# Scaling and adding 32 gathered rows on GpSimd instead of VectorE in a fused expert block

## What is computed

```python
q = (xb @ w_query).reshape(PEER_TOKEN_BLOCK, PEER_HEADS, 2, D_KEY // 2)
...
sc, ci = lax.top_k(cand, PEER_TOPK)
e = (jnp.take_along_axis(i1, ci // PEER_TOPK, axis=-1) * N_KEYS
     + jnp.take_along_axis(i2, ci % PEER_TOPK, axis=-1))
g = jax.nn.softmax(sc, axis=-1)
u = expert_u[e]
act = jax.nn.gelu(jnp.einsum('td,thkd->thk', xb, u).astype(jnp.float32))
return jnp.einsum('thk,thkd->td', (g * act).astype(xb.dtype), expert_v[e])
```

## Time and profile before

| what | value |
|---|---|
| median of 3 runs | 1208.1 us (1206.0 to 1208.2) |
| the profiled execution's own time | 1209.2 us |
| its span, first to last instruction | 1207.1 us |
| PE busy over the span | 98% |
| DVE, ACT, POOL busy over the span | 63%, 58%, 61% |
| the down product | about 547 to 882 us |
| in it: PE, DVE, ACT, POOL busy | 329.1, 238.7, 177.1, 91.1 of 335 us |
| granted TensorE clock in it | 1.00 (the upper level, 2.4 GHz) |

### The profile page before, as it was taken

One profiled execution on the slowest core, in us unless ns is written; L12 is line 12 of the kernel. 1 busy time (PEld: TensorE's weight loads), 2 busy tenths in 40 slices (PEclk: granted clock), 3 DMA queues, 4 the chain that ended last, 5 costly groups with the idle time before them and its releaser, 6 DMA issues.

```text
span 1207.1 us, 24649 instructions
## 1 busy us (share of the span) xinstructions
PE 1179.2 (98%) x8981; PEld 1111.7 (92%) x8981; DVE 759.0 (63%) x1516; ACT 704.3 (58%) x1370; POOL 741.8 (61%) x349
## 2 busy tenths in 40 slices
PE   7999999999999999999999999999999999999997
PEld 6888999999999999999899999999999988899896
DVE  4454059995007778885777777777647746457446
ACT  5585445556558888775555555555564666456554
POOL 7747868888887777774232232331057776677674
PEclk9999999999999999999999999999999999999999
DMA  6735545665554444457778778777665434454443
GB/s 243 264 122 192 179 139 193 203 203 198 199 203 169 168 170 167 165 174 274 251 264 270 262 254 272 249 255 256 195 236 192 140 126 137 140 203 149 136 158 108
DMA packets 67145, 237.68 MB, mean 197 GB/s; under 512 B 8912, under 2 KB 10360, under 8 KB 66688
## 3 DMA queue, kind: packets, MB, share of 16 engines
q1 hardware_dynamic: 57024, 206.14, 50.9%
q0 software_dynamic: 7392, 25.68, 5.9%
q10 hardware_dynamic: 2656, 4.90, 1.1%
HBM read 232.30 MB, written 6.31 MB: 198 GB/s over the span
## 4 chain that ended last, share of the span: by engine, by line
PE 82%; DMA 5%; DVE 4%; ACT 4%; POOL 2%; issue 2%; DVEq 0%; SPq 0%; ACTq 0%
PE W L581 29%; PE W L825 6%; PE A L825 6%; PE A L625 5%; PE A L632 5%; PE A L627 5%; DMA ring<-exp_v 4%; PE A L827 3%; PE W L827 3%; PE A L605 2%; PE A L610 2%; PE A L606 2%; POOL ringl L490 2%; PE W L867 2%; ACT ringh L1316 1%
## 5 line engine op out<-in xcount | busy, mean ns | idle before, releaser
L490 POOL TENSOR_TENSOR ringl<-ring,ringh 128x1024 fp32r<-128x1024 f32 x137 | 341.6, 2514 | 132.4 <-ACT ringh L1120 112.9
L520 POOL TENSOR_TENSOR ringl<-ring,ringh 128x1024 fp32r<-128x1024 f32 x126 | 302.0, 2398 | 76.9 <-ACT ringh L1316 42.6
L581 PE MATMUL W<-XTh,ringh 128*128 128x256 f32 x1024 | 287.6, 281 | 0.1
L581 PE MATMUL W<-XTl,ringh 128*128 128x256 f32 x1024 | 282.8, 276 | 0.0
L581 PE MATMUL W<-XTh,ringl 128*128 128x256 f32 x1024 | 282.7, 276 | 0.0
L1316 ACT ACTIVATE ringh<-ring 128x1024 fp32r<-128x1024 f32 x181 | 190.5, 1053 | 34.9 <-DMA ring<-exp_v 32.6
L1120 ACT ACTIVATE ringh<-ring 128x1024 fp32r<-128x1024 f32 x135 | 141.7, 1058 | 116.3 <-PE A L632 47.2
L1769 DVE TENSOR_TENSOR ringl<-ring,ringh 128x1024 fp32r<-128x1024 f32 x127 | 155.4, 1224 | 69.2 <-ACT ringh L1316 61.3
L581 PEld LDWEIGHTS W<-XTh,ringh 128*128 128x128 f32 x1024 | 192.3, 188 | 0.3 <-ACTq L1227 0.3
L581 PEld LDWEIGHTS W<-XTl,ringh 128*128 128x128 f32 x1024 | 192.4, 188 | 0.0
L581 PEld LDWEIGHTS W<-XTh,ringl 128*128 128x128 f32 x1024 | 192.2, 188 | 0.0
(11 more groups left out here) (298 smaller groups left out, 2254.6 us busy)
## 6 DMA issues: line engine op xcount, KB each, us to landing
ring<-exp_u SPq DMA_DIRECT2D x128, 512.0 KB
ring<-exp_v SPq DMA_DIRECT2D x128, 512.0 KB
ring<-w SPq DMA_DIRECT2D x72, 512.0 KB
ring<-w_out SPq DMA_DIRECT2D x24, 512.0 KB
ring<-w_in SPq DMA_DIRECT2D x20, 512.0 KB
ring<-w_query SPq DMA_DIRECT2D x16, 512.0 KB
skewed<-scratch POOLq DMA_DIRECT2D x1, 2048.0 KB, 11.6
H<-lng POOLq DMA_DIRECT2D x2, 1024.0 KB, 6.5
```

Source lines behind the costliest of these rows:

```text
L490: pool.tensor_tensor(ringl[:, slot, :], ring[:, slot, :], ringh[:, slot, :].bitcast(F32), ALU.subtract)\
L520: pool.tensor_tensor(ringl[:, slot, :], ring[:, slot, :], ringh[:, slot, :].bitcast(F32), ALU.subtract)\
L581: last = pe.matmul(dst, stationary[a], moving[b], start=start and n == 0, stop=stop and n == 2, skip_group_check=True)
```

## The change

`added_after` and `add_gathered` are gone from DVE's stream. POOL now waits for PE's columns itself (`unit_used`, at 6 + 18g/5 finished columns), computes the factor, and does in two instructions what DVE did in one: a product into the gather's own buffer and an addition to `ACC`. Each of its instructions waits for the one before by a semaphore. After the addition it starts the two indirect DMAs of gather g+3. DVE's stream keeps `column_low` and `next_low` alone.

```diff
-            for g in range(GATHER_SLOTS, GATHERS):
-                pool.wait_ge(gath_used, g - GATHER_SLOTS + 1)
-                gather_kept(g)
-                gather_rows(g)
+            pool.wait_ge(gq_in, 16 * GROUPS)
+            for g in range(GATHERS):
+                slot = g % GATHER_SLOTS
+                pool.wait_ge(unit_used, U_DOWN + FIRST_ADDED + 18 * g // 5)
+                pool.wait_ge(gath_in[slot], 16 * (g // GATHER_SLOTS + 1))
+                pool.wait_ge(zd_in[slot], 16 * (g // GATHER_SLOTS + 1))
+                pool.tensor_tensor(GA[:, g:g + 1], ZD[:, g:g + 1], GQ[:, g:g + 1], ALU.mult).then_inc(zd_gated, 1)
+                pool.wait_ge(zd_gated, g + 1)
+                rows_in = GATHERED[slot]
+                pool.tensor_tensor(ACC if g == 0 else rows_in, rows_in, GA[:, g:g + 1].broadcast_to([P, D]), ALU.mult)\
+                    .then_inc(gath_scaled, 1)
+                if g:
+                    pool.wait_ge(gath_scaled, g + 1)
+                    pool.tensor_tensor(ACC, ACC, rows_in, ALU.add).then_inc(gath_used, 1)
+                    pool.wait_ge(gath_used, g + 1)
...
+                if g + GATHER_SLOTS < GATHERS:
+                    gather_kept(g + GATHER_SLOTS)
+                    gather_rows(g + GATHER_SLOTS)
...
-            def add_gathered(g):
-
-                dve.wait_ge(gath_in[g % GATHER_SLOTS], 16 * (g // GATHER_SLOTS + 1))
-                dve.wait_ge(zd_in[g % GATHER_SLOTS], 16 * (g // GATHER_SLOTS + 1))
...
-                dve.tensor_tensor(GA[:, g:g + 1], ZD[:, g:g + 1], GQ[:, g:g + 1], ALU.mult).then_inc(zd_gated, 1)
...
-                    dve.scalar_tensor_tensor(out=ACC, in0=rows_in, scalar=gate, in1=ACC, op0=ALU.mult, op1=ALU.add)\
-                        .then_inc(gath_used, 1)
...
                 if u < U_LAYER + 1:
                     next_low(u + 1, u % SLOTS)
-                if added_after(n) is not None:
-                    add_gathered(added_after(n))
```

More of the change, by code:

```diff
@@ L188, in gated_before @@
     return TD if j == AMID - 1 else 4 * min(FIRST_AMID + j + 2, QUADS)
-def added_after(col):
-    when = [FIRST_ADDED + 18 * k // 5 for k in range(GATHERS)]
-    return when.index(col) if col in when else None
 def units_through(g):
@@ L390, in program @@
         gath_in = [sem(f"gath_in{n}") for n in range(GATHER_SLOTS)]
-        gath_used = sem("gath_used")
+        gath_used, gath_scaled = sem("gath_used"), sem("gath_scaled")
         r1_ready, pair_done = sem("r1_ready"), sem("pair_done")
@@ L543, in _ @@
                 gather_kept(g)
-            for g in range(GATHER_SLOTS, GATHERS):
-                pool.wait_ge(gath_used, g - GATHER_SLOTS + 1)
-                gather_kept(g)
-                gather_rows(g)
+            pool.wait_ge(gq_in, 16 * GROUPS)
[13 more added lines that the diff above has]
+                    pool.wait_ge(gath_used, g + 1)
+                else:
+                    pool.wait_ge(gath_scaled, 1)
+                    pool.nop().then_inc(gath_used, 1)
+                if g + GATHER_SLOTS < GATHERS:
+                    gather_kept(g + GATHER_SLOTS)
+                    gather_rows(g + GATHER_SLOTS)
             pool.wait_ge(unit_used, U_LAYER)
@@ L1775, in column_low @@
                     .then_inc(hl_done, 1)
-            def add_gathered(g):
-                dve.wait_ge(gath_in[g % GATHER_SLOTS], 16 * (g // GATHER_SLOTS + 1))
-                dve.wait_ge(zd_in[g % GATHER_SLOTS], 16 * (g // GATHER_SLOTS + 1))
-                if g == 0:
-                    dve.wait_ge(gq_in, 16 * GROUPS)
-                dve.tensor_tensor(GA[:, g:g + 1], ZD[:, g:g + 1], GQ[:, g:g + 1], ALU.mult).then_inc(zd_gated, 1)
-                dve.wait_ge(zd_gated, g + 1)
-                rows_in, gate = GATHERED[g % GATHER_SLOTS], GA[:, g:g + 1]
-                if g:
-                    dve.wait_ge(gath_used, g)
-                if g == 0:
-                    dve.tensor_scalar(ACC, rows_in, gate, None, ALU.mult).then_inc(gath_used, 1)
-                else:
-                    dve.scalar_tensor_tensor(out=ACC, in0=rows_in, scalar=gate, in1=ACC, op0=ALU.mult, op1=ALU.add)\
-                        .then_inc(gath_used, 1)
             dve.wait_ge(gate_dve, 2 + QUADS)
```

## The result

The changed kernel takes 1251.8 us (median of four runs, 1251.6 to 1255.4), the kernel before 1208.15 in the same measurement (1206.0 to 1213.6). The ratio is 1.036, with a 95% interval of 1.032 to 1.040. So the change costs 43.7 us. The forecast was 1265 and the range 1230 to 1290: the sign and the mechanism hold, the size was too large by 13 us.

What follows compares the result with a forecast made beforehand. PE, busy 98% of the span, was taken to bound the kernel. Losses of 62.9 us over the gathers less 5.7 us of removed waits gave +57.2 on 1209.2, so 1266.4, or 1265 us as median; range 1230 to 1290.

Steps and rivals of the forecast that it cites:

- That DVE and POOL exclude each other, and in turns: Down product: two-SBUF-input DVE instructions and POOL tensor instructions alternate, one each; about 2.0 us lost per gather.
- no taking of turns: Rival, down product: POOL keeps SBUF for product and addition together, 3.4 us lost per gather, 1308 us; chance 0.05.
- POOL's instructions at 3.5 us when behind a `next_low`: Expected sign in the profile after: POOL's product and addition take 2.4 us when free, 3.5 behind a `next_low`.
- Two waits per gather, not one: Down product: PE waits for `column_low` after both product and addition, taken as 2.0 us per gather.
- product first: Case where POOL's product starts ahead of `column_low`: PE loses 0.9, then 1.2 us behind the addition, sum 2.1.
- The product at 2.41 us: POOL's product of 128x1024 by the gate, taken to last as long as an addition with two full inputs: 2.41 us.
- The rival with a cheap product: Down product: POOL's product takes 1.41 us, so 1.1 us is lost per gather, +28 us, 1237; chance 0.15.
- The credit of 5.7 us for PE's waits of before: Down product: all 5.7 us that PE waited for `column_low` in eight places subtracted as won, the most possible.
- these waits have two sources that meet: PE's eight waits, 5.7 us: ACT gets its unit late from a load, and DVE is adding when `column_low` falls due.
- POOL itself too slow: Rival, down product: loss about 2.3 us per gather and POOL's backlog reaches the fold, 1290 us at most; chance 0.13.
- The fold at no cost: End of the down product: 17.5 us remain for the 6.4 the last gather needs, so the fold costs nothing more.
- a gain of 5.7 us: Rival, down product: POOL holds DVE up for less than 1.3 us, PE's waits go, 1202 us; chance 0.05.

Runs made afterwards that it cites:

- writes_only: The changed kernel with POOL's product and addition replaced by four memsets of the same buffers per gather; ratio 0.9955 to the kernel before.
- no_refill: The changed kernel without the row transfers of gathers 3 to 31, product and addition kept; ratio 1.031 to the kernel before.
- factor_only: The changed kernel without products and additions on POOL, factors and all gathers kept; ratio 0.998 to the kernel before.
- split4: The changed kernel with POOL's product and addition each cut into four pieces of 128x256; ratio 1.029 to the kernel before.
- product_only: The changed kernel without POOL's additions, factor and product kept; ratio 1.005 to the kernel before.

## Why the prediction was right in kind and 13 us too high

**That DVE and POOL exclude each other, and in turns: right.** The evidence came from the stage behind this one, and it held in a stage that had never had POOL work. `column_low` and `next_low` went to maxima of 2.1 and 3.4 us with medians unchanged, and writes_only shows that it is POOL's reads that do it. The predicted manner (one instruction each, the held one ending shortly after) is the timeline at 659 us, to 0.1 us. There the short `column_low` gets in between product and addition, which rules out the rival "no taking of turns" (1308). One expected sign is missing: POOL's instructions at 3.5 us when behind a `next_low`. In the change the turns cost DVE much and POOL's two instructions hardly anything (the product 2.14 at most, the addition 2.43), since POOL's addition follows its product within 0.1 us:

```profile
L551 POOL TENSOR_TENSOR H<-H x31: 2383/2419/2429, 576.0 to 896.0; 128x1024 f32<-128x1024 f32 x31
```

**Two waits per gather, not one: right.** 0.41 and 1.13 were measured where the case "product first" had 0.9 and 1.2. The addition's row is the forecast's (2.42 against 2.41), and so is the second wait.

**The product at 2.41 us: the step that failed.** It takes 1.89:

```profile
L547 POOL TENSOR_TENSOR H<-H,RB x32: 1893/1894/2139, 564.8 to 894.1; 128x1024 f32<-128x1024 f32 x32
```

The bounds were 1.41 and 2.41, and the upper one was taken since DVE shows no gain from a repeated input. POOL does show one, halfway. The 0.52 us shorten the first wait by as much. In the terms of the sum: 62.9 us were forecast as lost in all gathers and 52.3 were measured, which is 10.6 of the 13.3 us of error. The short product alone makes 32 x 0.52 = 16.6 us less; what the forecast left out, the restart of 0.10 per gather and the 2.5 us of the transfers, gives some 6 us back. The rival with a cheap product (1237) had the cause right and the amount wrong; the truth lies between the two.

**The credit of 5.7 us for PE's waits of before: too small as a number to subtract, and only in part right as a reading.** It was put down to DVE being freed. The other 2.7 us of the error are that a wait costs more than the idle time its row shows (the restart, 0.26 us for each of the eight, and a few stops too short to be counted), so that 8.4 us were lost before, not 5.7. The old waits are indeed gone from the total, because every step now loses more than they did and late loads hide beside the hold-ups (no_refill: only 2.5 us). But with DVE freed and nobody in its way there were still 9.7 us lost and 5.1 us of waits (factor_only, with the transfers at another place) and 4.6 us lost in writes_only. The sentence "these waits have two sources that meet" holds for two of the eight, 1.65 us; the other six have one source, a late load. The profile held a hint: DVE's stream had 31 additions, alike and evenly spaced, and PE only eight waits, while ACT waited 28 times for loads.

**Smaller terms.** The factor takes 0.36 on average, not 0.25, and up to 0.95 when behind a DVE instruction; POOL sees PE's count 0.25 after the column's start, 0.11 before ACT. The two cancel. The own waits are 0.07 to 0.1, as assumed. The DMAs stand where they were put, the small one at 1.59 us on average, and POOL still has 84.8 us of idle time: "works almost without pause" was too dark, by the shorter product and by DMAs that were not all held up. So the rival "POOL itself too slow" (1290) is ruled out for the change.

**The fold at no cost: right.** The last addition starts at 896.0, and PE does not wait. split4 shows what it would have been if POOL had run short: 25.1 us in one piece.

**The balance.** 31 steps at 1.64 are 50.8, and 1.5 come outside them: 52.3 lost. Less the 8.4 of before this gives +43.9, measured +43.7.

**Why it couldn't win.** The most that taking the additions off DVE brought in any run is what writes_only shows: 3.8 us in the stage and a ratio of 0.9955. The forecast gave 0.05 to a gain of 5.7 us. Its condition was that POOL hold `column_low` up for less than 1.3 us; by the sum found in product_only, an instruction that starts 0.58 after its column may take 2.2 - 0.58 = 1.6 us before PE notices. The product at 1.89 misses that by 0.3, the addition by 0.8.

## What to carry to other kernels

Before moving elementwise work from DVE to POOL, look at what the remaining DVE instructions read: if they have two SBUF inputs, POOL's work is not beside theirs but in turn with it, and each POOL instruction must fit into the slack of the next short DVE instruction that someone waits for. The number to compare is one instruction's duration with that slack, not the two engines' busy shares; cutting into pieces helps until POOL, which pays for every instruction and waits its turn too, runs out of time itself. And before crediting an engine's waits to the work that is to be removed, look at each wait: does that work stand directly in front of it, and what made it late?

## What the runs showed of the hardware that was not expected

- A POOL tensor_tensor over 128x1024 with one input repeated from a single number per partition takes 1.89 us, with two full inputs 2.42; on DVE there is no such difference. A POOL memset of that size takes 0.95 and holds up nothing.
- An instruction of POOL cut in four does not take a quarter: 0.61 (product) and 0.72 (addition) at its shortest, 0.89 and 0.95 on average in split4 beside a busy DVE, so 7.4 us for what takes 1.89 + 2.42 = 4.3 in two pieces.
- Starting an indirect DMA takes POOL 0.95 us in the kernel before when no two-input DVE instruction runs (13 of 64), and up to 1.99 when a `next_low` has just begun: mostly it then ends 0.82 after that instruction does.
- After a wait PE is behind by more than the idle time: the first matmul takes 0.47 in place of 0.37, and the column after it 2.61 in place of 2.51. At 581.23 in the kernel before, PE was idle for 0.62 us, its column came 0.78 late, and the next took 0.10 more.
- The share of a resource in the chain of waits can be large (DMA 14%) and its removal worth next to nothing (no_refill, 2.5 us in the stage), when it ends beside something else.
